# Two attention cores of a two-layer block: work of the next gate in their tails, later sigmoids, a split value product, an earlier exponential table

## The reference, cut to what matters

```python
# branch 1: mLSTM, 4 heads of 256, two directions
num, den = (decay weights * q k^T) v          # exp() of gate sums
y_ml = rmsnorm_per_head(num / den) * ml_head_g * sigmoid(o)
# branch 2: differential attention, 8 heads of two 64-wide halves
p = softmax(q1 k1^T / 8) - lam * softmax(q2 k2^T / 8)
y_da = rmsnorm_per_head(p v) * da_head_g * (1 - lam_init)
# branch 3: Fourier mixing
merged = sum(sigmoid(h @ w_gate_i) * (y_i @ w_branch_i))
x = x + gain * (merged @ w_out)
```

## Time and profile before

| | us |
|---|---|
| median of 3 runs | 3055.8 (3055.72 to 3056.21) |
| profiled execution, its own time | 3056.91 |
| its span, first to last instruction | 3054.8 |
| TensorE busy | 2983.3 |
| VectorE busy | 1780.8 |
| ScalarE busy | 598.3 |
| GpSimd busy | 537.2 |

### The profile page before, as it was taken

One profiled execution on the slowest core, in us unless ns is written; L12 is line 12 of the kernel. 1 busy time (PEld: TensorE's weight loads), 2 busy tenths in 40 slices (PEclk: granted clock), 3 DMA queues, 4 the chain that ended last, 5 costly groups with the idle time before them and its releaser, 6 DMA issues.

```text
span 3054.8 us, 37651 instructions
## 1 busy us (share of the span) xinstructions
PE 2983.3 (98%) x15358; PEld 2250.3 (74%) x15358; DVE 1780.8 (58%) x2606; ACT 598.3 (20%) x1182; POOL 537.2 (18%) x214
## 2 busy tenths in 40 slices
PE   8999999999999999999999999999999999999998
PEld 4448898764458757886688888888888888678543
DVE  6994742657766555667853368777324503742574
ACT  2103222221121112113601131110021201511110
POOL 4330000023332001221021112211110001010332
PEclk9999999999999999999999999999999999999999
DMA  6663301355543302442021234444232143133453
GB/s 265 229 240 138 139 31 57 115 197 172 196 165 127 108 28 76 156 150 67 28 97 56 83 145 159 148 140 145 95 134 84 65 159 107 56 152 135 158 177 126
DMA packets 57115, 389.86 MB, mean 128 GB/s; under 512 B 9072, under 2 KB 23408, under 8 KB 36336
## 3 DMA queue, kind: packets, MB, share of 16 engines
q1 hardware_dynamic: 52592, 383.27, 35.1%
q10 hardware_dynamic: 4352, 4.20, 0.7%
HBM read 373.53 MB, written 1.05 MB: 123 GB/s over the span
## 4 chain that ended last, share of the span: by engine, by line
PE 87%; DVE 9%; issue 2%; ACT 2%; DMA 0%; DVEq 0%; SPq 0%; ACTq 0%
PE bank L1140 86%; DVE small L3816 1%; DVE weights L3157 1%; PE bank L1143 1%; DVE arena L3486 0%; DVE factors L3170 0%; DVE factors L3065 0%; ACT h_T L2261 0%; DVE arena L3826 0%; DVE weights L3160 0%; DVE h_T L3259 0%; PE bank L1147 0%; DVE arena L3187 0%; DVE arena L3004 0%; DVE arena L3837 0%
## 5 line engine op out<-in xcount | busy, mean ns | idle before, releaser
L1140 PE MATMUL bank<-h_T,weights 128*128 128x256 f32 (+1 forms) x3184 | 779.4, 398 | 14.8 <-ACT arena L2378 3.1
L1140 PEld LDWEIGHTS bank<-h_T,weights 128*128 128x128 f32 x3184 | 601.9, 192 | 149.1 <-issue 63.1
L2876 POOL TENSOR_TENSOR weights<-weights 128x1024 f32<-128x1024 f32 (+2 forms) x105 | 274.1, 2611 | 1280.5 <-DMA weights<-wide_slabs_dram 1182.6
L2887 POOL TENSOR_TENSOR factors<-weights 128x1024 f32<-128x1024 f32 (+2 forms) x105 | 265.1, 2524 | 1208.8 <-PE bank L1140 984.6
L1140 PE MATMUL bank<-arena,weights 128*128 128x256 f32 x1784 | 394.0, 380 | 2.6 <-DVE arena L3187 1.0
L1140 PEld LDWEIGHTS bank<-arena,weights 128*128 128x128 f32 x1784 | 337.8, 190 | 51.9 <-DVE arena L3187 1.8
L1140 PE MATMUL bank<-weights,h_T 128*128 128x256 f32 (+2 forms) x1000 | 323.7, 470 | 4.3 <-DMA weights<-wide_slabs_dram 2.2
L1140 PE MATMUL bank<-factors,weights 128*128 128x256 f32 x1432 | 323.9, 379 | 4.0 <-DVE arena L3187 3.9
L1140 PE MATMUL bank<-weights,factors 128*128 128x256 f32 (+1 forms) x960 | 312.9, 470 | 3.8 <-DVE factors L3170 2.0
L1140 PEld LDWEIGHTS bank<-factors,weights 128*128 128x128 f32 x1432 | 271.6, 190 | 42.2 <-DVE arena L3187 5.1
L1140 PEld LDWEIGHTS bank<-weights,h_T 128*128 128x128 f32 x1000 | 190.3, 191 | 118.1 <-issue 89.8
(11 more groups left out here) (390 smaller groups left out, 2685.6 us busy)
## 6 DMA issues: line engine op xcount, KB each, us to landing
weights<-wide_slabs_dram SPq DMA_DIRECT2D x143, 2048.0 KB, 7.8
arena<-wide_slabs_dram SPq DMA_DIRECT2D x61, 512.0 KB, 4.2
weights<-down_slabs_dram SPq DMA_DIRECT2D x8, 1408.0 KB, 5.8
merged_T<-arena SPq DMA_DIRECT2D x240, 32.0 KB, 1.9
merged_T<-wide_slabs_dram SPq DMA_DIRECT2D x15, 512.0 KB, 4.4
x_T<-wide_slabs_dram SPq DMA_DIRECT2D x11, 512.0 KB, 9.3
arena<-arena ACTq DMA_DIRECT2D x16, 256.0 KB, 10.1
weights<-wide_slabs_dram SPq DMA_DIRECT2D x3, 1024.0 KB, 5.2
```

What stands on the lines that cost most here:

```text
L1140: return mm(out, lhsT, rhs, start=start, stop=stop, skip_group_check=True)
L2876: nc.gpsimd.tensor_tensor(b[2], b[2], b[3], ALU.add).then_inc(S["first_sums"], 1)
L2887: nc.gpsimd.tensor_tensor(e, b[2], b[0], ALU.subtract).then_inc(S["first_sums"], 1)
```

## The change

Five edits, in both layers unless a layer is named.

- *Last value product in halves.* P4 of the last mLSTM value unit is made with k 0 and 1 between the transposes and the wait for the column copies, and with k 2 and 3 after the scores. The first fill waits for the C11 join of that unit instead of for ScalarE's corner copy.
- *Next gate begun at the tails.* The mLSTM tail no longer waits for the last two outputs before gate0; in layer 0 the wait stands before P5 of gate0, in layer 1 before its third and fourth tile. In the other core P1 of gate1 (layer 1: its first tile) is made in four quarters (`gate1_begins`) in the three steps without scores and after them; the wait for the last outputs stands before the transposes.
- *Fills.* The fill of step 0 is made in step 1, behind its scores.
- *Sigmoids behind the copies* (layer 0). The sigmoids of `ml_o` and gate0 are made after the snaps of P5 and P6 of the next gate.
- *Table ahead.* An empty Exp on one element stands before the corner copy of the last value unit.

```diff
@@ -1437,13 +1437,15 @@
-            def run_units(keys, before, ready, frees=None):
+            def run_units(keys, before, ready, frees=None, begun=False):
                         owner = key
+                        if name == "P1" and i == 0 and begun:
+                            continue
                         if name == "P4":
@@ -1958,6 +1960,7 @@
                 last.then_inc(S["pe_for_dve"], 1)
+                product(run[-1], "P4", ks=range(2))
                 t.wait("dve_for_pe")
@@ -1993,8 +1996,8 @@
                     ml_scores(0, s)
-                end_units(run)
-                fill = filler(ST[p + "ml_o"], 1, lambda k: H2[:, k, 0:nq], nq, (S["act_out"], ST[p + "ml_v"].act_end))
+                product(run[-1], "P4", ks=range(2, 4))
+                fill = filler(ST[p + "ml_o"], 1, lambda k: H2[:, k, 0:nq], nq, (S["joined"], UNIT[run[-1]].join("C11")))
                 for h in range(4):
@@ -2010,7 +2013,11 @@
                         ml_values(h, d)
-                t.wait("pv_out", 2)
+                t.skip("pv_out", 2)
+                ml_out = t.at("pv_out")
+
+                def ml_banks_free():
+                    pe.wait_ge(S["pv_out"], ml_out)
@@ -2020,10 +2027,10 @@
                     run_units(run, {
-                        (proj0, "P1"): lambda: token_outputs_back(t, transpose, Y_ML, qtiles, 8),
+                        (gate0, "P5"): ml_banks_free, (proj0, "P1"): lambda: token_outputs_back(t, transpose, Y_ML, qtiles, 8),
                     }, {(proj0, "P2"): outputs_arrive}, frees={1: ("act_out", ST[p + "ml_o"].act_end)})
                 else:
-                    merge(p + "ml", H2, bT, nq, [("act_out", ST[p + "ml_v"].act_end), ("act_out", ST[p + "ml_o"].act_end)],
+                    merge(p + "ml", H2, bT, nq, [("act_out", ST[p + "ml_v"].act_end), ("act_out", ST[p + "ml_o"].act_end), ("pv_out", ml_out - 1), ("pv_out", ml_out)],
                           output=lambda: token_outputs_back(t, transpose, Y_ML, qtiles, 8))
@@ -2070,6 +2077,21 @@
                 per = 32 // len(units)
+                gate1 = p + "da_gate1", 0
+
+                def gate1_begins(part):
+
+                    if la == 0:
+                        product(gate1, "P1", ks=(part,))
+                        return
+                    st = ST[gate1[0]]
+                    if part == 0:
+                        arrived(st, 0)
+                    for k in (2 * part, 2 * part + 1):
+                        last = matmul(bank[0][:, 0:nq], wtile(st, 0, k), H2[:, k, 0:nq], start=k == 0, stop=k == KT - 1)
+                    if part == 3:
+                        last.then_inc(S["tile_done"], 1)
+
                 for n in range(len(units) + 3):
@@ -2077,13 +2099,20 @@
                             end_units(run)
-                        fill(per)
+                        else:
+                            fill(2 * per if n == 1 else per)
+                    else:
+                        if n == len(units):
+                            t.wait("probs_in")
+                        gate1_begins(n - len(units))
                     if n >= 3:
                         da_turn(n - 2)
-                t.wait("probs_in", 2)
-                t.wait("pv_out", 2)
+                gate1_begins(3)
+                t.wait("probs_in")
+                t.skip("pv_out", 2)
+                da_out = t.at("pv_out")
@@ -2103,9 +2132,13 @@
                     gate1, proj0, proj1, fn0, fn1 = run
-                    run_units(run, {
-                        (proj0, "P1"): lambda: token_outputs_back(t, transpose, 12288, qtiles, 8),
-                    }, {(proj0, "P2"): outputs_arrive}, frees={3: ("act_out", ST[p + "da_gate0"].act_end)})
+
+                    def da_outputs():
+                        pe.wait_ge(S["pv_out"], da_out)
+                        token_outputs_back(t, transpose, 12288, qtiles, 8)
+
+                    run_units(run, {(proj0, "P1"): da_outputs}, {(proj0, "P2"): outputs_arrive},
+                              frees={3: ("act_out", ST[p + "da_gate0"].act_end)}, begun=True)
                     pe.wait_ge(S["dft_consts"], 16 * (la + 1))
@@ -2114,7 +2147,8 @@
                 else:
-                    project(ST[p + "da_gate1"], lambda k: H2[:, k, 0:nq], nq, drains=by_act, frees=act_frees(p + "da_gate0"))
+                    project(ST[p + "da_gate1"], lambda k: H2[:, k, 0:nq], nq, drains=by_act, frees=act_frees(p + "da_gate0"), part=(1, 4))
+                    pe.wait_ge(S["pv_out"], da_out)
                     token_outputs_back(t, transpose, 12288, qtiles, 8)
@@ -2383,7 +2417,7 @@
-            def units_out(keys, before, middle, after):
+            def units_out(keys, before, middle, after, late={}):
@@ -2400,6 +2434,8 @@
                     snap(key, "s2", scale)
+                    if key in late:
+                        late[key]()
                     if "gate" in key[0]:
@@ -2700,6 +2736,8 @@
                     t.out(af(stat[:, 16:16 + 4 * qtiles], stat[:, 0:4 * qtiles], ACT.Sqrt), "act_for_dve")
+
+                def ml_sigmoids():
                     t.out(af(ML_O[:, :, 0:nq], ML_O[:, :, 0:nq], ACT.Sigmoid), "act_for_dve")
@@ -2720,15 +2758,17 @@
                     units_out(run, {gate1: gates_free(p + "ml_gate1")},
-                              {gate0: ml_roots, k0: turn_q, v0: turn_k}, {})
+                              {gate0: ml_roots, k0: turn_q, v0: turn_k}, {}, late={gate0: ml_sigmoids})
                 else:
                     ml_roots()
+                    ml_sigmoids()
                     merge(p + "ml", nq, base=ML_GATES)
                     units_out(run, {}, {run[2]: turn_k}, {})
+                t.step(af(stat[0:1, 138:139], ones[0:1, 0:1], ACT.Exp))
                 corner(run[-1])
@@ -2769,16 +2809,19 @@
                     t.out(af(stat[:, 64:64 + 8 * qtiles], stat[:, 32:32 + 8 * qtiles], ACT.Sqrt), "act_for_dve")
+
+                def da_sigmoids():
                     t.out(af(DA_GATES0[:, :, 0:nq], DA_GATES0[:, :, 0:nq], ACT.Sigmoid), "act_for_dve")
                     gate1, proj0, proj1, fn0, fn1 = run
-                    units_out(run, {}, {gate1: da_roots}, {})
+                    units_out(run, {}, {gate1: da_roots}, {}, late={gate1: da_sigmoids})
                     corner(fn1)
                     da_roots()
+                    da_sigmoids()
                     merge(p + "da", nq, base=DA_GATES, halves=(1,))
```

## The result

The changed kernel takes 3037.4 us (median of 4 runs, 3036.2 to 3039.35) where the kernel before took 3056.0 beside it (3055.72 to 3056.21): a ratio of 0.9941, interval 0.9929 to 0.9953. Part of the 18.6 is the kernel before itself: beside the later experiments its median was 3054.4 (13 runs), 3055.0 (25) and 3055.5 (9), and the changed kernel once more took 3038.3, 16.1 us less than the first of these. The ratio barely moves (0.9943).

A forecast was written before the change was run, and what follows sets the result against it. TensorE was taken to bound the kernel, busy 2983.3 of 3054.8 us, so gains come only from its idle time. Eight terms sum to 14.2 us, taking the 3055.8 median to 3041.6; range 3038.5 to 3046.5.

The forecast's parts named there:

- seven of eight terms: Gains at head and tail of the mLSTM and attention cores in both layers; all eight sum to 14.2 us.
- the moved wait of the mLSTM tail: Layer 0: the 1.29 us wait moves behind two products where its banks are free, 1.44 us of a 2.0 term.
- S4's wait before P3: Layer 0 attention tail: P3 waits 1 us for weight sum S4, leaving 1.8 us gained before POOL's effect.
- The attention head of layer 0: VectorE works 1.2 us earlier but is still held up by POOL's addition; 0.2 us gained, between 0 and 1.2.
- The wall missed: Layer 0 attention head: the wall is POOL's addition holding up a VectorE operation; missing it was priced at 1.2 us.
- The landing doesn't move: Layer 0 attention head: weights landing sets POOL's start; the load follows the last value product, which doesn't move.
- POOL stands elsewhere: Rival on both POOL-VectorE encounters: 1.0 + 0.3 us more gained, 3040.3, or 3044 if S4 is hit; chance 0.09.
- The slices of before are all at full level: Argument against the rival of 1.5% less clock from denser TensorE work after 1040 us, 3071.8; chance 0.04.
- Between the cores every stage shows TensorE without a wait: Stages between cores: gains are carried along, 0 us change; new waits there would show the prediction wrong.
- DVE-paced heads: Rival: at all four core heads DVE and ScalarE refill the gaps, 6.2 us less gained, 3047.8; chance 0.11.
- quarters that don't fit: Rival: in both attention tails quarters delay values as much as they fill, 2.3 us less, 3043.9; chance 0.08.
- the table dropped: Case: the corner's copy drops the Exp table again; 1.28 us less in the last core's head at most.

The follow-up runs named there:

- the changed kernel with the addition held: Changed kernel, GpSimd's addition beside layer 0's attention head held until gate1's first product; 3042.9 us, ratio 0.9952.
- before with the addition held: Kernel before, GpSimd's addition beside layer 0's attention head held until gate1's first product; 3055.3 us, ratio 1.0003.
- part 3: Edits alone on the kernel before: halves 3051.5, fills with table 3052.7, table 3055.5, tails 3051.5, sigmoids 3054.9; changed kernel with sigmoids back 3043.9 us.
- its second profile: The changed kernel unaltered, run again for another profile; 3038.3 us, ratio 0.9943.
- the kernel with S3 moved: Changed kernel, with VectorE making weight sum S3 before its wait for the squares in layer 0's attention tail; 3039.9 us, ratio 0.9944.
- part 5: No kernel of its own: profiles compared for half-clock stretches, waits between the cores and POOL meeting VectorE behind the last core.

## Why the prediction was right or wrong

**Direction, and seven of eight terms: right.** Together they were forecast at 14.0 and measured at 14.92; each is off by 0 to 0.34. Alone, the halves gave 4.21 of 4.21, layer 1's attention head 1.87 of 1.88 and its tail 3.30 of 3.32, so these stand by themselves. Layer 0's two tails don't.

**The mechanisms of the tails: right in sum.** The working had 1.44 for the moved wait of the mLSTM tail and 0.54 for the late sigmoid. Alone they are 0 and 0.55, together 2.11 (1.98 forecast): the 1.44 is there only once the sigmoid stands behind the copy. In layer 0's attention tail the text took the sigmoid to lie beside P3 and P7. It does so only because it was moved: left in place it costs 0.78. S4's wait before P3 was foretold as 1 us and is 1.02; POOL did go ahead of the multiply, with 2.36 for its addition instead of 4.81:

```profile
1516.28 2.36 POOL L2930 TENSOR_TENSOR factors<-weights 128x1024 f32<-128x1024 f32 x1 [97.50 <-DVE weights L3203]
1516.87 6.05 DVE L3897 TENSOR_TENSOR arena<-arena,small 128x4096 f32<-128x4096 f32 x1
```

The multiply began beside it and took 6.05 instead of 4.42, as the working allowed when it had the multiply wait for the addition.

**The attention head of layer 0: the step that failed.** The prediction put it at 0.2, between 0 and 1.2, by this reasoning: VectorE's work comes 1.2 us earlier, POOL's start is set by the landing "which doesn't move", so VectorE reaches the wall earlier and leaves it at the same time. It measured 2.04 in the changed kernel's profile. Two things in it were wrong.

- *The upper bound.* "The wall missed" was priced as the 1.2 us of earlier work alone. But before itself pays 1.24 us at the wall (1.41 for 0.17), and a run that misses it gets that back too: 1.2 + 1.24 = 2.4, which is what the changed kernel with the addition held gained (2.42). With that bound the changed kernel could have been put at 3039.4 by the forecast's other terms, and the range would have reached a microsecond or so further down. The 1.2 itself stands (2.42 - 1.24, or 2.42 - 1.04 = 1.38 against before with the addition held).
- *The landing doesn't move.* It moved by 1.0 to 1.35 us, in every kernel with the early Exp, as the runs of part 3 showed, because a packet of instructions slid into the load. The wall then stands not at 7.70 but at 8.7 to 9.05 after the issue, and what it hits is a matter of tenths: 0.38 us lost in the changed kernel's profile, 2.08 in its second, 2.17 in the kernel with S3 moved.

No kernel had the new order with the old landing, so what the head gives with it isn't shown. An estimate from the rows: 7.70 us after the issue the addition would have started at 1414.75, half a microsecond ahead of the scalar operation at 1415.23. That is how it stood in the kernel with the early Exp alone, which lost 1.53 us to it, so the head would have given some 0.9 us, within the term's 0 to 1.2. That the changed kernel's profile shows 2.04 is then the later landing together with the luck of what stood there; in its second profile, by the same luck, the term came out at 0.34, near the forecast.

The Trainium skill (Advanced Engine Details and Errata, GPSIMD Details) says that Pool conflicts with DVE instructions in a 2-port mode or with two SBUF inputs. The stretched rows agree in kind: scalar operations from SBUF to SBUF (0.41 to 2.40) and one on two SBUF inputs (0.75 to 2.83), never the maxima that read a bank. What I drew from it, a term near 0, did not follow: the rule tells which operations are blocked, not which of them happens to stand there, and a bank-reading maximum of 1.42 us took most of the addition in the changed kernel's profile. The rival "POOL stands elsewhere" named this, with a chance of 0.09 and 1.0 us for the head. Of the six profiles with the early Exp and the addition not held, three lost 0.5 or less and three 1.5 or more: it should have been an even chance, at 1.8 us.

**The rest of the miss.** The eight stages that were changed give 16.96 us in the changed kernel's profile and 15.27 in the second. Against the 14.2 forecast the first profile has 3.1 us more: 1.8 in the failed term, 0.9 in the other seven, 0.3 where nothing was changed. The second has 3.3 more, and there the failed term is 0.14 of them and the unchanged stretches 2.2. So the mis-sized term is the larger part of the miss in one profile and hardly any in the other, and for the executions without a profile the split is open. The unchanged stretches are mostly clock: 1.47 and 2.94 ahead of the first edit, -0.96 and -0.82 between the cores. Between the cores 0.35 to 0.43 us is gained up to 1608 by every kernel but one, those with one edit alone too, so it belongs to the profile of before; behind that 1.0 and 1.9 us are lost near 1800, as part 5 has it, and near 2220, where the clock falls too, another 0.4 is lost in the first profile and 0.6 won back in the second. A range that allows nothing for this is too narrow: the two ends of the head alone move the time by some 2 us, and the clock adds another 1.5 either way.

**"The slices of before are all at full level": too coarse.** The page shows nine tenths in all 40 slices, but a slice is 76 us long; the windows of 10 to 20 us show 0.83 and 0.91. The rival that rested on it (a clock lower by 1.5% through denser work) did not come: the mean granted clock is 0.995 in the changed kernel (0.994 in before), and in no profile under 0.993.

**"Between the cores every stage shows TensorE without a wait": wrong.** Before has waits of 1.27, 1.01, 0.88 and 0.58 us between 1640 and 1810 alone. And the prediction's own sign of being wrong, new waits between the cores, is there: the 1.14 us for VectorE's sum (L3213), 0.34 in the second profile. What the cores gained was not all carried along.

**DVE-paced heads, quarters that don't fit, the table dropped:** none of the three came. The heads gave 2.61, 1.60 and 1.88 in every profile with all edits (to 0.02), the tails 3.32 (more than forecast), and the first exponential follows the corner's copy without a load.

## What to carry to other kernels

When a stall is likely to be missed or hit by tenths, price both ends with the stall that the kernel before already pays, and give each its own chance. A step's price may be in another queue's order: the same move was worth 0 or 2.11 us, by whether ScalarE's copy stood behind a sigmoid. And compare stages by partner instructions and not by the end: the stages repeat to 0.02 us where whole times differ by 3 and more.

## What the runs showed of the hardware

- Packets of instructions come through the DMA engines that carry the data. One of 16 KB, 0.96 us long, inside a load of 2 MB put the end of its data off by 0.9 to 1.3 us (7.24 in before, 8.18 to 8.55 us after the issue in the nine profiles with the early Exp); one added instruction on ScalarE was enough to bring it there.
- A POOL addition of 2.35 us (2.3 to 2.8 in the rows) held the VectorE operation without a bank among its operands that met it, until the addition had ended: 0.17 to 1.41, 0.41 to 2.40, 0.42 to 2.61, 0.55 to 2.08, 0.75 to 2.83 and 2.92. Maxima that read a bank ran beside it in their usual 1.42 us. In layer 0's attention head one operation was paid for per addition, at 0.4 to 2.2 us.
- The clock falls to half level for a few microseconds at a time, at a few places where TensorE has just waited 0.5 to 2.5 us, in some runs of identical code and not in others. The start of the first edit moved by up to 3.2 us with it. Where VectorE sets the pace it costs less: near 1800 such a stretch cost 0.2 us when it began 0.7 us ahead of VectorE's chain, and 1.2 when it began 2.9 ahead.
